# Gathered rows of a PEER layer taken in among its one-hot steps, on one Trainium2 core

## Chip, core and metric

One core of one Trainium2 chip runs the whole program. The metric is device microseconds, the median of several executions; a difference below about 0.2% can't be told from none. Engines are TensorE (PE in the profile), VectorE (DVE), ScalarE (ACT), GpSimd (POOL) and SyncE (SP), which issues most DMAs.

## What is computed

Two transformer blocks over 512 tokens of width 1024, ending in a feed-forward layer with 16384 experts. Only this layer (`peer_block`) is touched:

```python
q = (xb @ w_q).reshape(T, 8, 2, 128)
s = einsum('thpd,hpkd->thpk', q, sub_keys)        # 128 keys per half
sv, si = top_k(s, 16)
cand, cidx = sums and index pairs of the 16 x 16 candidates
top_s, pos = top_k(cand, 16)                      # 8 heads x 16 experts per token
gate = softmax(top_s)
u = take(expert_u, eidx); act = gelu(einsum('thkd,td->thk', u, xb))
v = take(expert_v, eidx); out = einsum('thk,thkd->td', gate * act, v)
```

Here T is the tokens, h the heads, k the 16 chosen experts.

## The kernel before

The layer is done in two ways. For the first 128 tokens (`GT`) the 128 chosen rows of `expert_u` and then the 128 of `expert_v` are gathered by indirect DMAs, one row per token and DMA (128 x 1024 floats, 0.5 MB): GpSimd issues them (`row_load`, L2847), VectorE reduces each (`gd`, L2598: a multiply with a sum for `expert_u`, a multiply-add for `expert_v`). That makes 256 rows, in four buffers `grow`, loaded three ahead.

For the other 384 tokens (`SD`) all experts are computed: 128 blocks of `expert_u` (128 experts each) are multiplied with the tokens, passed through Gelu, multiplied by a gate matrix that is zero except for the chosen experts, and multiplied with `expert_v`. Weights are loaded by SP into three ring buffers (`load_to`). Every fp32 weight block is split into a high and a low part: ScalarE copies it as the high part (`hi`, L1302 to L1306), the low part is the difference, made by GpSimd (`lo_to`, L2691 to L2697) or VectorE (`lo`, L1803 to L1806) as `by_pool` says. TensorE does three matmuls per product (`mm3`, L804 to L806). Up to the block `FIRST` there are three slots (`SLOTS`) for split blocks: `hi(n)` waits until TensorE has used block n - 3 (`slot_before`); after it there are eight.

The order of the work is one list, `ORDER`, written by `schedule`; each engine walks it and does its own part of every piece, in that order. `walk` also calls, after every piece in `one_unit` ("pre" is one), the engine's split function for two blocks ahead:

```python
for name, *args in ORDER:
    if name in pieces:
        pieces[name](*args)
    if name in one_unit:
        split_to(args[-1] + 2)
```

The stages, in order:
- Routing (`cand`, `best`, `gates`, `decode`, `look`, `sums`, `soft`, four blocks of 128 tokens): VectorE finds the chosen experts. `soft(0)` gives `eidx`, the indices of the gathered rows. Among this TensorE does `pre` pieces: `pre(j)` is block j of `expert_u` (24 matmuls of 384 columns), whose Gelu ScalarE writes to a tile that SP stores to DRAM (`zd`). There are 80 `pre` in all; 20 (`SOFT`) are done before `oh_begin`.
- One-hot (`hot(tb)`, 24 steps of 16 tokens): VectorE makes five bf16 products of 128 x 2048 (L2571, L2573, three times L2576), TensorE 48 matmuls (L1212) that turn them into gate rows, ScalarE moves those to a staging tile (L1707, four times a step), SP stores a piece of `TG` = 64 tokens every fourth step (`gd`, six pieces of 4 MB). Two `pre` stand before each `hot`; 52 `pre` (`HOT`) are in this stage, four of them before the first `hot`.
- Passage: after `ex_begin` (all engines wait for all) eight `pre`, the first gate loads (`gload`), `xtok` (the first 128 tokens turned to rows, `gx`, on TensorE and ScalarE), `gfirst` (the first three row loads), and `z(0)`.
- Expert loop, c = 0 to 31 with four blocks each: `z(c, j)` multiplies the stored (c < 20) or just computed (c >= 20) Gelu by the gates on VectorE (L2589), ScalarE and GpSimd split the result (L1728, L2843), `v(c, j)` multiplies it with a block of `expert_v` (18 matmuls of 512 columns). `feed(share)` puts `gd` pieces in between: 1.2 per `v` up to c = 18, then 1.8 per `z` and 1.8 per `v`.

Of the kernel before, what the change touches and what calls it, by code (L numbers as in the profile page):

```python
# [23 lines left out]
TG = 64  # L24
# [12 lines left out]
SOFT = 4 + 4 * 4  # L37
HOT = 4 + 48
# [109 lines left out]
def placed(items, kind):  # L148
    assert len(items) == len(PLACES[kind])
    return list(zip(PLACES[kind], items))  # L150


def schedule():
# [300 lines left out]
def build(nc, t):  # L454
    ORDER, UNITS, FIRST, OF = schedule()
    NU = len(UNITS)
    with ExitStack() as ctx:
# [168 lines left out]
        a = Stage("oh")  # L626
        iom = a(128 * QT, BF16)
# [7 lines left out]
        a = Stage("ex")  # L635
        exw = a(2048)
# [3 lines left out]
        gall = a(2 * JC * SD)  # L640
# [4 lines left out]
        grows = a(GR * 1024)  # L645
        gx = a(1024)
# [26 lines left out]
        whole = {n for n, (name, _) in enumerate(UNITS) if name == "ada"}  # L673
        halved = [n for n in range(FIRST) if n not in whole]
# [623 lines left out]
        def scalar_program(act):  # L1298
# [479 lines left out]
            def xg(k):  # L1778
# [14 lines left out]
                  **{f"{s}_begin": lambda s=s: fence(w, A, s) for s in ("rw", "eo", "at", "ao", "mx", "pk", "oh", "ex")}}, hi_to)  # L1793

        def vector_program(dve):
# [867 lines left out]
            def last():  # L2663
                w.wait_ge(tensor_done, T("bc", "ng"))
                for k in range(KT):
# [13 lines left out]
                  "yms": yms, "wo": wo, "wq": ahead_of, "keys": keys, "pre": lambda j, n: lo_to(n + 1), "cand": cand_,  # L2679
# [4 lines left out]
        def pool_program(pool):  # L2684
            w = Once(pool)
            at = {"lo": 0}
# [159 lines left out]

            def row_load(e):  # L2847
                if e >= NG:
                    return
# [5 lines left out]
                pool.indirect_dma_start(grow[e % GR], None, rows, bass.IndirectOffsetOnAxis(ap=at_, axis=0)).then_inc(  # L2855
                    grow_in[e % GR], 16)

            def gfirst():
                for s in st_out:
                    w.wait_ge(s, 16 * (SD // TG // 2))  # L2860
                for e in range(GR - 1):
                    row_load(e)
# [4 lines left out]
                  "pre": ahead_of, "z": z, "v": v, "gfirst": gfirst, "gd": lambda e: row_load(e + GR - 1),  # L2867
# [302 lines left out]
```

## Time and profile before

| | us |
|---|---|
| median of 3 runs | 2854.35 (2854.25 to 2856.07) |
| the profiled execution, its own time | 2859.36 |
| its span | 2857.5 |
| TensorE busy | 2697.9 (94%) |
| VectorE busy | 2213.6 (77%) |
| GpSimd busy | 1298.4 (45%) |
| ScalarE busy | 1212.2 (42%) |
| mean granted TensorE clock | 0.981 |

The sums cover stages with different limits, so each stage is to be read alone. The page also gives the busy share over 40 slices of 71 us; the routing stage, the one-hot stage and the passage are slices 22 to 28, the expert loop is 28 to 38:

```
PE   8889999999999999999999799999999999998987
DVE  3688888876878977657569998883777788888975
DMA  7321111134422221023233346677999999899961
```

### The profile page before, as it was taken

What the parts mean: (1) busy time and instruction counts of PE and PEld (TensorE: products, weight loads), DVE (VectorE), ACT (ScalarE), POOL (GpSimd) and SP (SyncE); (2) the same over time, 40 slices, a digit from 0 to 9 for tenths busy, and PEclk for the clock granted to TensorE, in tenths of its full rate; (3) what the DMA queues carried; (4) which work ended last, traced back from release to release, by engine and by line L of the source; (5) the groups of instructions that cost most, each with busy time, mean ns of one, the idle gap of its engine ahead of it and who ended that gap; (6) DMA issues with size and microseconds to landing.
All of it is one profiled execution on the core that took longest, in us unless ns stands there. A gap on an engine that the chain in (4) does not pass through costs nothing.

```text
span 2857.5 us, 36824 instructions
## 1 busy us (share of the span) xinstructions
PE 2697.9 (94%) x14355; PEld 2240.7 (78%) x14355; DVE 2213.6 (77%) x3528; ACT 1212.2 (42%) x1802; POOL 1298.4 (45%) x827
## 2 busy tenths in 40 slices
PE   8889999999999999999999799999999999998987
PEld 4567777767767788787788799999888898777765
DVE  3688888876878977657569998883777788888975
ACT  4234444443533466733334446564333333233333
POOL 2233333332224544204444455555676766667730
PEclk9999999999999999999999899999999999999998
DMA  7321111134422221023233346677999999899961
GB/s 280 103 70 53 52 52 52 52 125 151 144 67 74 82 67 45 30 83 117 82 103 103 119 133 225 209 249 278 360 377 361 376 341 340 321 337 322 325 246 37
DMA packets 163165, 496.12 MB, mean 174 GB/s; under 512 B 15152, under 2 KB 50992, under 8 KB 162864
## 3 DMA queue, kind: packets, MB, share of 16 engines
q1 hardware_dynamic: 126128, 359.53, 37.2%
q0 software_dynamic: 36864, 134.23, 12.7%
q8 instruction: 114, 1.87, 0.3%
q14 instruction: 59, 0.48, 0.0%
HBM read 443.90 MB, written 49.81 MB: 173 GB/s over the span
## 4 chain that ended last, share of the span: by engine, by line
PE 50%; DVE 24%; DMA 12%; ACT 7%; issue 4%; POOL 3%; SPq 1%; DVEq 0%; ACTq 0%; POOLq 0%
PE ps L804 12%; PE ps L806 12%; PE ps L805 12%; DMA ex<-in_ev,small 4%; DMA ex<-in_urow,small 4%; DVE ex L1806 3%; PE ps L1212 2%; DVE ex L2589 2%; DVE ex L2603 2%; DVE ex L2610 2%; DVE wsp L1806 2%; PE ps L977 2%; POOL ex L2843 1%; PE ps L997 1%; DMA ring<-in_ev 1%
## 5 line engine op out<-in xcount | busy, mean ns | idle before, releaser
L2697 POOL TENSOR_TENSOR wsp<-ring,wsp 128x1024 fp32r<-128x1024 f32 x219 | 568.2, 2600 | 867.5 <-ACT wsp L1306 839.7
L804 PE MATMUL ps<-hT,wsp 128*128 128x512 f32 (+1 forms) x2040 | 780.7, 383 | 38.0 <-POOL wsp L2697 20.0
L806 PE MATMUL ps<-hT,wsp 128*128 128x512 f32 (+1 forms) x2040 | 752.4, 369 | 0.0
L805 PE MATMUL ps<-hT,wsp 128*128 128x512 f32 (+1 forms) x2040 | 752.0, 369 | 0.0
L804 PEld LDWEIGHTS ps<-hT,wsp 128*128 128x128 f32 x2040 | 388.4, 190 | 109.1 <-issue 32.1
L806 PEld LDWEIGHTS ps<-hT,wsp 128*128 128x128 f32 x2040 | 387.8, 190 | 46.7
L805 PEld LDWEIGHTS ps<-hT,wsp 128*128 128x128 f32 x2040 | 388.9, 191 | 44.0 <-issue 5.0
L1306 ACT ACTIVATE wsp<-ring 128x1024 fp32r<-128x1024 f32 x317 | 331.9, 1055 | 158.0 <-PE ps L806 80.0
L804 PE MATMUL ps<-ex 128*128 128x512 f32 x588 | 233.7, 397 | 30.4 <-DVE ex L1806 26.9
L2855 POOL DMA_INDIRECT ex<-in_ev,small x128 | 190.5, 1488 | 110.1 <-DVE ex L2610 93.1
L2855 POOL DMA_INDIRECT ex<-in_urow,small x128 | 197.1, 1540 | 88.6 <-DVE small L2603 77.3
L805 PE MATMUL ps<-ex 128*128 128x512 f32 x588 | 230.5, 392 | 0.0
L806 PE MATMUL ps<-ex 128*128 128x512 f32 x588 | 229.9, 391 | 0.0
L1306 ACT ACTIVATE ex<-ring 128x1024 fp32r<-128x1024 f32 x115 | 120.3, 1060 | 252.9 <-DMA ring<-in_ev 188.5
L2610 DVE SCALAR_TENSOR_TENSOR ex<-ex,small 128x1024 f32<-128x1024 f32 x127 | 171.5, 1351 | 40.7 <-DMA ex<-in_ev,small 31.0
L1806 DVE TENSOR_TENSOR ex<-ring,ex 128x1024 fp32r<-128x1024 f32 x115 | 175.3, 1526 | 34.8 <-ACT ex L1306 34.8
L1982 DVE SCALAR_TENSOR_TENSOR ps<-rw,vec,ps 128x512 f32<-128x512 f32 x232 | 173.4, 747 | 5.3
L2603 DVE CUSTOM_DVE_ANT_0 ex<-ex 128x1024 f32<-128x1024 f32 x128 | 159.0, 1253 | 23.4 <-DMA ex<-in_urow,small 23.0
L2576 DVE TENSOR_TENSOR oh<-oh,px 128x2048 bf16<-128x2048 bf16 x72 | 176.2, 2500 | 0.8
L804 PEld LDWEIGHTS ps<-ex 128*128 128x128 f32 x588 | 111.1, 189 | 63.9 <-DVE ex L1806 41.6
L2843 POOL TENSOR_TENSOR ex<-ex 128x384 fp32r<-128x384 f32 x128 | 143.0, 1136 | 37.4 <-ACT ex L1728 36.5
L1728 ACT ACTIVATE ex<-ex 128x384 fp32r<-128x384 f32 x128 | 64.8, 525 | 199.4 <-DVE ex L2589 199.4
(431 smaller groups left out, 4909.3 us busy)
## 6 DMA issues: line engine op xcount, KB each, us to landing
ring<-in_eu SPq DMA_DIRECT2D x128, 512.0 KB
ring<-in_ev SPq DMA_DIRECT2D x128, 512.0 KB
ring<-in_ein SPq DMA_DIRECT2D x57, 512.0 KB
gd<-oh SPq DMA_DIRECT2D x6, 4096.0 KB, 14.0
ex<-gd SPq DMA_DIRECT2D x32, 768.0 KB
ring<-in_oin SPq DMA_DIRECT2D x39, 512.0 KB
ring<-in_ada SPq DMA_DIRECT2D x30, 512.0 KB
ex<-zd SPq DMA_DIRECT2D x20, 768.0 KB, 9.9
```

The lines of the kernel that those rows point to most:

```text
L804: pe.matmul(out, W[0], R[0], start=first, stop=False)
L805: pe.matmul(out, W[0], R[1], start=False, stop=False)
L806: return pe.matmul(out, W[1], R[0], start=False, stop=last)
L1306: act.activation(split_of(n)[:, 0, :], raw_of(n), ACT.Copy).then_inc(scalar_done, A.step("hi", n))
L1806: dve.tensor_tensor(s[:, 1, :], raw_of(n), s[:, 0, :].bitcast(F32), ALU.subtract).then_inc(vector_done, V.step("lo", n))
L1982: dve.scalar_tensor_tensor(out=y, in0=u[:, k:k + S], scalar=col("conv_w", m * TAPS + k), in1=taps, op0=ALU.mult, op1=ALU.add).then_inc(vec ...
L2576: dve.tensor_tensor(by_two(g), by_two(oj), spread_(i, t0), ALU.mult).then_inc(vector_done, V.step("hot", tb))
L2603: dve.tensor_tensor_reduce(out=row, in0=row, in1=gx, scale=1.0, scalar=0.0, op0=ALU.mult, op1=ALU.add, accum_out=of).then_inc(vector_done, ...
L2610: dve.scalar_tensor_tensor(out=gx, in0=row, scalar=of, in1=gx, op0=ALU.mult, op1=ALU.add).then_inc(vector_done, V.step("g", e))
L2697: pool.tensor_tensor(s[:, 1, :], raw_of(i), s[:, 0, :].bitcast(F32), ALU.subtract).then_inc(pool_done, G.step("lo", i))
L2843: pool.tensor_tensor(agb[c % 2][:, 1, j, :], exg[2 + (c * JC + j) % 3], agb[c % 2][:, 0, j, :].bitcast(F32), ALU.subtract).then_inc(pool_d ...
L2855: pool.indirect_dma_start(grow[e % GR], None, rows, bass.IndirectOffsetOnAxis(ap=at_, axis=0)).then_inc(grow_in[e % GR], 16)
```

## The change

Seven things:
- 40 of the 256 rows (`EARLY`) are taken earlier: one `gd` after every `hot`, four after the last, twelve in the passage. Until then they use three buffers, two ahead (`AHEAD`); `row_slots` gives buffer, count and predecessor of each row. Fewer are left for the loop: `feed` shares of 0.95 and 1.58.
- `xtok` moves to the start of the routing stage, `gfirst` (two rows) behind its first block.
- `TG` is 48: eight stored pieces of 3 MB, one every third step.
- 28 `pre` in the routing stage rather than 20, 44 in the one-hot stage rather than 52 (five before the first `hot`, then one or two per `hot`).
- `by_pool` gives the low parts of blocks 33 to 71 to VectorE; its `pre` handler asks for block n rather than n + 1 there.
- The tiles are placed anew, so that `gx` and three row buffers are free from the routing stage on.
- ScalarE waits for the stores of the first staging tile at `ex_begin`, no longer in `xtok`; `gload` waits for the `zd` stores.

```diff
-TG = 64
+TG = 48
-SOFT = 4 + 4 * 4
-HOT = 4 + 48
+EARLY = 40
+AHEAD = 2
+SOFT = 6 + 5 + 5 + 6 + 6
+HOT = 5 + 24 + 15
+def row_slots():
+    late = [3, *((EARLY + i) % 3 for i in range(3))]
+    slot = [e % 3 if e < EARLY else late[(e - EARLY) % GR] for e in range(NG)]
+    nth = [slot[:e].count(slot[e]) for e in range(NG)]
+    before = [max((k for k in range(e) if slot[k] == slot[e]), default=-1) for e in range(NG)]
+    return slot, nth, before
...
     for _ in range(4):
         pre()
+    order.append(("xtok",))
+    for _ in range(2):
+        pre()
     for blk in range(4):
         order.append(("cand", blk))
         pre()
         for part in range(4):
             order.append(("best", blk, part))
-            if part in (1, 3):
+            if part:
                 pre()
...
         pre()
+        if blk > 1:
+            pre()
         order.append(("sums", blk))
         order.append(("soft", blk))
+        if blk == 0:
+            order.append(("gfirst",))
...
     order.append(("oh_begin",))
-    for _ in range(4):
+    for _ in range(5):
         pre()
     for tb in range(SD // TB):
         pre()
-        pre()
+        if tb % 8 in (1, 3, 5, 6, 7):
+            pre()
         order.append(("hot", tb))
+        early(1)
+    early(4)
...
     order.append(("ex_begin",))
     pre()
+    early(2)
     pre()
+    early(1)
     order.append(("gload", 0))
     pre()
+    early(2)
     order.append(("gload", 1))
     for _ in range(3):
         pre()
-    order += [("xtok",), ("gfirst",)]
+        early(2)
     order.extend(zs(0))
     pre()
+    early(1)
     pre()
...
-        share = 1.2 if c < NPRE - 1 else 1.8
+        share = 0.95 if c < NPRE - 1 else 1.58
...
-                    or name == "eu" and u < NPRE * JC)
+                    or name == "eu" and u < NPRE * JC and not SOFT + 5 <= u < SOFT + HOT)
...
+            def ex_begin():
+                fence(w, A, "ex")
+                w.wait_ge(st_out[0], 16 * (SD // TG // 2))
...
-                  "pre": lambda j, n: lo_to(n + 1), "cand": cand_,
+                  "pre": lambda j, n: lo_to(n if SOFT + 5 <= j < SOFT + HOT else n + 1), "cand": cand_,
...
-                if e >= GR:
-                    w.wait_ge(vector_done, V("g", e - GR))
+                if row_before[e] >= 0:
+                    w.wait_ge(vector_done, V("g", row_before[e]))
...
             def gfirst():
-                for s in st_out:
-                    w.wait_ge(s, 16 * (SD // TG // 2))
-                for e in range(GR - 1):
-                    row_load(e)
+                rows_to(AHEAD - 1)
...
-                  "gd": lambda e: row_load(e + GR - 1),
+                  "gd": lambda e: rows_to(e + (AHEAD if e < EARLY - 1 else GR - 1)),
...
             def gload(c):
+                for s in z_out:
+                    w.wait_ge(s, 16 * ((SOFT + HOT) // 2))
```

## Rows read from the trace of the kernel before

**Rows 1.** The page of before: its first line and section 1.

```profile
span 2857.5 us, 36824 instructions
...
PE 2697.9 (94%) x14355; PEld 2240.7 (78%) x14355; DVE 2213.6 (77%) x3528; ACT 1212.2 (42%) x1802; POOL 1298.4 (45%) x827
```

**Rows 2.** Windows cut at the stages (columns in the first line).

```profile
core 0: us, PE busy (x) PEld busy (x) DVE busy (x) ACT busy (x) POOL busy (x), PEclk, DMA share, GB/s
1549.00:1666.20 117.20, 91.19 (x496) 90.32 (x495) 111.95 (x419) 47.93 (x70) 50.77 (x20) 0.89 0.39 124
1691.00:1950.40 259.40, 259.40 (x2259) 255.78 (x2257) 220.16 (x113) 155.87 (x188) 142.12 (x46) 1.00 0.65 211
1950.40:1992.00 41.60, 37.08 (x224) 36.47 (x223) 6.51 (x7) 17.03 (x25) 21.28 (x13) 1.00 0.92 333
1992.00:2304.00 312.00, 311.92 (x1354) 255.43 (x1355) 245.03 (x324) 112.62 (x152) 221.29 (x163) 0.99 0.98 367
2304.00:2744.00 440.00, 404.88 (x2002) 357.63 (x2001) 387.26 (x352) 139.39 (x189) 300.11 (x214) 1.00 0.92 330
```

**Rows 3.** Timeline of VectorE, 1985 to 1995 (start us, us, engine, line).

```profile
1989.32 2.36 DVE L1806 TENSOR_TENSOR ex<-ring,ex 128x1024 fp32r<-128x1024 f32 x2 [1.54 <-ACT ex L1306]
```

**Rows 4.** The chain that ended last (start us, us, what).

```profile
1936.40 2.77 PE ps L1212 x48
...
1947.55 2.77 PE ps L1212 x48
...
2019.34 7.83 DMA ex<-in_urow,small
```

**Rows 5.** Timeline of ScalarE, and of GpSimd for 1953.43.

```profile
1623.61 0.49 ACT L1673 ACTIVATE pk<-ps 128x384 f32<-128x384 f32 x1 [2.72 <-PE ps L806]
...
1627.77 0.49 ACT L1673 ACTIVATE pk<-ps 128x384 f32<-128x384 f32 x1 [2.72 <-PE ps L806]
...
1948.30 3.82 ACT L1707 ACTIVATE oh<-ps 128x512 f32<-128x512 f32 x4 [0.21 <-PE ps L1212]
1952.20 1.06 ACT L1306 ACTIVATE wsp<-ring 128x1024 fp32r<-128x1024 f32 x1
...
1953.43 2.39 POOL L2697 TENSOR_TENSOR wsp<-ring,wsp 128x1024 fp32r<-128x1024 f32 x1 [6.10 <-ACT wsp L1306]
```

**Rows 6.** The line of the one-hot products on VectorE.

```profile
L2576 DVE TENSOR_TENSOR oh<-oh,px x72: 1209/3408/3429, 1676.4 to 1934.9; 128x2048 bf16<-128x2048 bf16 x72
```

**Rows 7.** Windows of 5 us, 1985 to 2000.

```profile
1985.00:1990.00 5.00, 3.80 (x22) 3.48 (x21) 3.01 (x2) 2.19 (x3) 3.36 (x4) 1.00 0.87 351
1990.00:1995.00 5.00, 2.92 (x7) 2.38 (x8) 4.10 (x6) 3.39 (x7) 2.21 (x3) 0.71 0.64 207
1995.00:2000.00 5.00, 5.00 (x22) 4.08 (x22) 5.00 (x4) 2.54 (x3) 4.85 (x3) 0.95 1.02 405
```

**Rows 8.** Timeline of TensorE: `xtok`.

```profile
1976.74 3.73 PE L1224 MATMUL ps<-ident,hT 128*128 128x128 f32 x32
```

**Rows 9.** Timeline of VectorE, routing stage: where blocks 2 and 3 begin.

```profile
1612.99 0.98 DVE L2466 TENSOR_TENSOR pk<-pk 128x128 f32<-128x128 f32 x5
...
1637.92 0.98 DVE L2466 TENSOR_TENSOR pk<-pk 128x128 f32<-128x128 f32 x5
```

**Rows 10.** Windows of routing blocks 1 and 2.

```profile
1591.80:1613.00 21.20, 7.08 (x41) 6.76 (x40) 20.50 (x89) 3.86 (x6) 4.86 (x2) 0.76 0.33 104
1613.00:1637.90 24.90, 18.79 (x99) 18.50 (x99) 24.17 (x88) 10.60 (x16) 9.92 (x4) 0.91 0.37 116
```

**Rows 11.** Groups by form, VectorE, 2305 to 2745.

```profile
L2610 DVE SCALAR_TENSOR_TENSOR ex<-ex,small 128x1024 f32<-128x1024 f32 x124 | 167.1, 1348 | 40.4 <-DMA ex<-in_ev,small 31.0 <-DVE wsp L1806 0.3
...
L2603 DVE CUSTOM_DVE_ANT_0 ex<-ex 128x1024 f32<-128x1024 f32 x41 | 54.0, 1329 | 12.2 <-DMA ex<-in_urow,small 12.1
```

**Rows 12.** Timeline, 2545 to 2550: GpSimd's issue, and VectorE beside it.

```profile
2547.29 1.93 POOL L2855 DMA_INDIRECT ex<-in_ev,small  x1 [1.96 <-DVE ex L2610]
...
2545.73 2.68 DVE L2610 SCALAR_TENSOR_TENSOR ex<-ex,small 128x1024 f32<-128x1024 f32 x2
```

More of the change, by code:

```diff
@@ L380, in schedule, with early @@
         pre()
+        if blk > 1:
+            pre()
         order.append(("sums", blk))
         order.append(("soft", blk))
+        if blk == 0:
+            order.append(("gfirst",))
+    row = [0, 0.0]
+    def early(n):
+        for _ in range(n):
+            order.append(("gd", row[0]))
+            row[0] += 1
     assert z[0] == SOFT
     order.append(("oh_begin",))
-    for _ in range(4):
+    for _ in range(5):
         pre()
@@ L403, in schedule @@
         pre()
-    order += [("xtok",), ("gfirst",)]
+        early(2)
     order.extend(zs(0))
     pre()
+    early(1)
     pre()
+    assert row[0] == EARLY
     assert z[0] == NPRE * JC
     first = len(units)
-    row = [0, 0.0]
     def feed(share):
@@ L626, in build @@
         a = Stage("oh")
+        a(4 * 1024)
         iom = a(128 * QT, BF16)
@@ L635, in build @@
         a = Stage("ex")
+        gall = a(2 * JC * SD)
+        gr = a((GR + 1) * 1024)
         exw = a(2048)
@@ L673, in build @@
         whole = {n for n, (name, _) in enumerate(UNITS) if name == "ada"}
+        row_slot, row_nth, row_before = row_slots()
         halved = [n for n in range(FIRST) if n not in whole]
@@ L1792, in scalar_program @@
                   "v": v, "xtok": xtok, "gact": gact, "vl": vl, "vev": vev, "vtr": vtr, "pp": lambda m: pp(m) if m < 2 else None, "ple": lambda m, n: hi_to(n + 2), "ple_ev": ple_ev, "ple_end": ple_end, "xg": xg,
-                  **{f"{s}_begin": lambda s=s: fence(w, A, s) for s in ("rw", "eo", "at", "ao", "mx", "pk", "oh", "ex")}}, hi_to)
+                  **{f"{s}_begin": lambda s=s: fence(w, A, s) for s in ("rw", "eo", "at", "ao", "mx", "pk", "oh")}, "ex_begin": ex_begin}, hi_to)
         def vector_program(dve):
@@ L2598, in gd @@
             def gd(e):
-                row, of = grow[e % GR], gact_[:, e % 128:e % 128 + 1]
-                w.wait_ge(grow_in[e % GR], 16 * (e // GR + 1))
+                row, of = grow[row_slot[e]], gact_[:, e % 128:e % 128 + 1]
+                w.wait_ge(grow_in[row_slot[e]], 16 * (row_nth[e] + 1))
                 if e < NG // 2:
@@ L2678, in vector_program @@
                   "pool_in": ahead_of, "mx_begin": mx_begin, "pool_ev": pool_ev, "bc": bc, "res": res, "vc": vc,
-                  "yms": yms, "wo": wo, "wq": ahead_of, "keys": keys, "pre": lambda j, n: lo_to(n + 1), "cand": cand_,
+                  "yms": yms, "wo": wo, "wq": ahead_of, "keys": keys, "pre": lambda j, n: lo_to(n if SOFT + 5 <= j < SOFT + HOT else n + 1), "cand": cand_,
                   "best": best, "gates": gates, "decode": decode, "look": look, "soft": soft, "hot": hot, "z": z, "v": v, "gd": gd, "gact": gact, "vl": vl, "vtr": vtr,
@@ L2685, in pool_program @@
             w = Once(pool)
-            at = {"lo": 0}
+            at = {"lo": 0, "row": 0}
             def own():
@@ L2845, in gated, with rows_to @@
                     pool_done, G.step("ag", c, j))
+            def rows_to(n):
+                while at["row"] <= min(n, NG - 1):
+                    row_load(at["row"])
+                    at["row"] += 1
             def row_load(e):
-                if e >= NG:
-                    return
                 w.wait_ge(vector_done, V("eidx"))
-                if e >= GR:
-                    w.wait_ge(vector_done, V("g", e - GR))
+                if row_before[e] >= 0:
+                    w.wait_ge(vector_done, V("g", row_before[e]))
                 rows = t["urow"][:, :] if e < NG // 2 else t["ev"].rearrange("i j d -> (i j) d")
                 at_ = eidx[:, e % 128:e % 128 + 1].bitcast(U32)
-                pool.indirect_dma_start(grow[e % GR], None, rows, bass.IndirectOffsetOnAxis(ap=at_, axis=0)).then_inc(
-                    grow_in[e % GR], 16)
+                pool.indirect_dma_start(grow[row_slot[e]], None, rows, bass.IndirectOffsetOnAxis(ap=at_, axis=0)).then_inc(
+                    grow_in[row_slot[e]], 16)
             def gfirst():
-                for s in st_out:
-                    w.wait_ge(s, 16 * (SD // TG // 2))
-                for e in range(GR - 1):
-                    row_load(e)
+                rows_to(AHEAD - 1)
             walk({"ada": ahead_of, "dense": dense_part, "norm_nf": norm_nf, "mix": mix,
@@ L2866, in pool_program @@
                   "qi": qi_, "key": key, "keyhi": keyhi, "value": ahead_of, "q": ahead_of, "turnq": turnq, "qhi": qhi, "gate": ahead_of, "quiet": quiet, "ogs": ogs,
-                  "pre": ahead_of, "z": z, "v": v, "gfirst": gfirst, "gd": lambda e: row_load(e + GR - 1),
+                  "pre": ahead_of, "z": z, "v": v, "gfirst": gfirst, "gd": lambda e: rows_to(e + (AHEAD if e < EARLY - 1 else GR - 1)),
                   **{f"{s}_begin": lambda s=s: fence(w, G, s) for s in ("rw", "eo", "at", "ao", "mx", "pk", "oh", "ex")}}, lo_to)
```

4 lines of the change are left out of this document (1 added, 3 removed).

## The prediction, made before the changed kernel ran

> **What bounds the kernel now.** I read the page's first section, then the windows cut at the stages, then in each stage the view that names its limit. [Rows 1]: the profiled span is 2857.5 us and TensorE is busy 94% of it, so time can only come from the places where it waits. [Rows 2] show these. In the routing stage (1549 to 1666) TensorE is busy 91.2 of 117.2 us at a granted clock of 0.89, and VectorE 112: the top-k blocks hold it. In the one-hot stage (1691 to 1950) TensorE is busy throughout and sets the pace; VectorE has 39 us of slack. The passage to the expert loop (1950 to 1992) is 41.6 us with the DMA share at 0.92. The first part of the expert loop (to 2304) is TensorE's again: 312 us for 76 `v` pieces, 4.1 us each. In the last part (to 2744) TensorE is idle 35 us, and DMA (0.92) and VectorE (88%) are both near full.
>
> **Two facts of the code that decide.** First, `walk` calls the split function with n + 2 after every `pre`, since "pre" is in `one_unit`; the handler's own n or n + 1 is overtaken by that. The trace shows it on VectorE: between the products of `z(0)` and of `z(1)` stand two low parts together [rows 3], where the handler's n + 1 alone would give one. So the edit of VectorE's `pre` handler does nothing, and at `pre(j)` VectorE makes the low part of block j + 2. Second, there are three split slots, so the high part of j + 2 waits until TensorE has used j - 1, and the low part waits for the high part.
>
> **Before**, these low parts are on GpSimd, beside everything. **After**, blocks 33 to 71 have theirs on VectorE, in program order: at step tb VectorE first makes the low part of jl + 2 (jl is the last block ahead of `hot(tb)`), and only then the five one-hot products of `hot(tb)`, for which TensorE waits. Those products can no longer run ahead. That is the wait that the change adds; behind it on VectorE are the products and the row's reduction, and TensorE waits for the products.
>
> **One-hot steps, term by term.** Now a step is two blocks and one `hot`: 11.15 us from one `hot` to the next, of which `hot` is 2.8 [rows 4]. A block is 4.16 us (from one Gelu to the next, [rows 5]).
> A product costs VectorE 1209 ns with GpSimd silent, and up to 3429 beside a GpSimd subtraction [rows 6]; GpSimd will have no subtraction here, so five cost 6.05. A low part costs 1.2 (two in 2.36, [rows 3]).
> A step with one block ahead of its `hot` (steps 2, 4, 8, 10, 12, 16, 18 and 20): ScalarE must first move out the last `hot`, which ends 4.57 us after that `hot` began (1952.12 against 1947.55), then makes the high part; a low part can begin at 1953.43, 5.88 us after [rows 4, 5]. Then 1.2 + 6.05 + 0.2 of signals: 13.3 us from `hot` to `hot`.
> A step with two blocks (15 of them): 2.8 + 4.16 to the use of block jl - 1, 0.2, then Gelu 0.49 and high part 1.06 (some 0.1 of them overlapped, [rows 5]), 0.2, low part 1.2, products 6.05, 0.16: 16.2 us.
> Sum of the 23 steps: 8 x 13.3 + 15 x 16.2 = 349 us, against 23 x 11.15 = 256: **+93**. Ends: +85 if signals and evictions overlap better, +100 if they don't. For the first `hot` TensorE has used five blocks at 20.8 us; high part, low part and products follow until 29.3, where TensorE would be ready at 25.0: **+4**.
> The 24 row reductions in these steps (1.3 us each) fall where VectorE waits for ScalarE, 5.9 us per step: 0. If that cover were gone, 31 us. Their loads are two steps ahead, some 28 us, against a landing of about 8 [rows 4]: 0. The stores in eight pieces rather than six are 768 bytes a packet and the same sum of bytes, at a lower demand per us than the DMA share of 0.65 of now [rows 2]: they hide, 0.
>
> **The clock.** Each step now leaves TensorE idle 5 to 6 us. After an idle time of 1.2 + 2.1 us around 1990 the granted clock reads 0.71 and then 0.95 in two slices of 5 us [rows 7]: at 1.2 GHz for a part, 5 x 0.29 + 5 x 0.05 = 1.7 us lost. The work that follows a gap is `hot`, which stands on the chain. 24 x 1.7 = **+41**; ends 0 (the clock stays at 2.4 GHz) and +65 (2.7 each).
>
> **Routing stage.** Eight more blocks here (28 for 20), and `xtok`, 3.7 us [rows 8]. TensorE's room is 26 us idle and some 5 of low clock, against 8 x 4.16 + 3.7 = 37: at least +6. But VectorE holds the stage. Its blocks begin at 1591.8, 1613.0 and 1637.9 [rows 9]: 21.2 us beside two low parts of GpSimd, 24.9 beside four [rows 10], so 1.85 per low part. Blocks 1, 2 and 3 go from two, four, four to about six each: 7.4 + 3.7 + 3.7 = **+15** (6 to 20). The two row loads after block 0 hold GpSimd's queue until `eidx` (1591.8) and 3 us more; it has then split up to block 11, which TensorE ends at 1549 + 12 x 4.16 + 3.7 = 1602.6, so nothing waits.
>
> **Passage to the expert loop.** `xtok` leaves (-3.7), the last store is a quarter smaller. But rows 26 to 39 stand here, in three slots, two ahead: three rows per landing (8 us), GpSimd's issue and low part between (4) and reduction (1.3), some 4 us a row. The fence of all engines now takes in row 27. GpSimd's low parts 74 to 79 stand behind row issues that wait for VectorE, and `z(0)` stands behind row 38. Stepped through, `v(0)` starts 57 us after the last `hot`, where it is 41.6 now [rows 2]: **+16** (0 to +25).
>
> **Expert loop.** First part: TensorE sets it, fewer rows change nothing: 0. Last part: 440 us, where 48 pairs of a block and a `v` piece need 48 x 8.26 = 396. Rows here go from 165 to 144. On VectorE 21 rows take 21 x 1.35 = 28 with them, and their share of the 43 us that it waits for row transfers, 5 [rows 11]: -33. By bytes, 21 x 0.524 MB of 145 MB at 330 GB/s is 33 us too. **-32**; ends -15 (the low parts' own waits on transfers stay) and -44 (the floor).
>
> **Sum**: 93 + 4 + 41 + 15 + 16 - 32 = +137. The profiled execution took 2859.4 us, 5.0 over the median of 2854.35; the difference is set on the median: 2991.
>
> **A rule weighed.** A row issue of GpSimd reads its indices in SBUF. [Rows 12]: an issue of 1.93 us stands beside two VectorE operations with two SBUF inputs that last 2.68 together, 1.34 each, as everywhere (mean 1348 ns in [rows 11]); so issues hold nothing up. The Trainium skill (SBUF — State Buffer, "Who interferes with whom") says that a VectorE instruction with two SBUF inputs contends with a GpSimd instruction that reads SBUF, and that the one that starts first keeps the port pair for its whole length. By that rule the issues too could block products; for the subtractions the trace agrees, for the issues it doesn't.
>
> **Rivals.**
> A. The low parts don't hold the products back, because high parts come earlier than I read. Then TensorE sets the steps: 8 x 7.0 + 15 x 11.15 = 223, -33; no clock loss; -33 + 15 + 16 - 32 = -34: 2820, **faster**. For it: the counts of blocks per step fit VectorE's work (6.05 + 1.63 x 1.2 + 1.3 = 9.3 us) to TensorE's 9.6. Against it: the slots, and [rows 3]. It decides where the gap at each `hot` is under 1.4 us.
> B. The clock stays at 2.4 GHz through the gaps, as it does in the last part, at 1.00 with 35 us idle in all [rows 2]: 2950.
> C. Row issues block the products after all, 24 x 1.4 us (0.94 to 1.93): +34, 3025. Against: [rows 12], and that an issue follows a reduction, when VectorE is idle.
> D. A, but with the passage at +25 and the last part giving nothing back: 15 - 33 + 25 = +7, about the same as before.
>
> **Chances.** Forecast 0.65, B 0.16, C 0.06, A 0.11, D 0.02. A measurement tells 0.2% (6 us) from no change; faster 0.11, same 0.02, slower 0.87. The range takes the low ends, 85 + 4 + 0 + 6 + 0 - 44 = +51, and the high ends, 100 + 4 + 65 + 20 + 25 - 15 = +199: 2905 to 3050. That holds B and C and leaves out A and D.
>
> **What would show it.** Right: in the changed profile `hot` to `hot` is 13 and 16 us by turns, TensorE waits some 5 us before L1212 on VectorE's products, a product falls to 1.2 us, the clock line dips in the one-hot slices, and the last part takes about 408 us. Wrong: `hot` to `hot` of 7 and 11 us with no idle time ahead of it (A), a clock of 1.00 there (B), or products well over 1.21 us (C). A last part of 440 us would say that rows did not matter there.

## The result and the profile after

The changed kernel takes 2963.96 us (2962.85 to 2965.5, four runs); the kernel before, on the same chip, 2855.21 (2854.25 to 2861.45, four runs). The ratio is 1.0375, 95% interval 1.0357 to 1.0393: slower by 3.75%, +108.75 us. Forecast were +137 and 2991, range 2905 to 3050.

The page of the changed kernel: span, section 1, four lines of section 2, two groups of section 5, one line of section 6. L1245 is the one-hot matmul, L1841 VectorE's low part, L1339 ScalarE's high part, L2606, L2608 and L2611 the one-hot products, L2638 the row reduction, L2893 the row issue, L837 to L839 `mm3`, L1740 ScalarE's move of the gate rows.

```profile
span 2962.2 us, 36778 instructions
...
PE 2723.1 (92%) x14355; PEld 2273.0 (77%) x14355; DVE 2176.5 (73%) x3567; ACT 1213.3 (41%) x1802; POOL 1163.2 (39%) x788
...
PE   8889999999999999999999967667799999999987
...
DVE  3688888877869977567598755556677777889875
...
PEclk9999999999999999999999998898899999999998
DMA  7221111134422211132325454555999988999971
...
L1841 DVE TENSOR_TENSOR wsp<-ring,wsp 128x1024 fp32r<-128x1024 f32 x137 | 172.1, 1257 | 201.3 <-ACT wsp L1339 201.2
...
L1245 PE MATMUL ps<-oh 128*128 128x128 bf16 x1152 | 100.9, 267 | 108.1 <-DVE oh L2611 108.1
...
gd<-oh SPq DMA_DIRECT2D x8, 3072.0 KB, 11.4
```

Against [rows 1]: five slices of the one-hot stage, at 9 before, read 6 and 7 for TensorE, and VectorE has fallen there as well (5 and 6). When both engines are idler than before, neither is the bound: each waits for the other in turn. L1841 names the first wait (201 us on ScalarE's high part, 151.8 of them in the one-hot stage, 36 times), L1245 the second (108 us on the last product).

Windows of the changed kernel at its stages: two routing blocks, one-hot stage, passage, and the two parts of the expert loop (columns as in [rows 2]).

```profile
1557.50:1600.00 42.50, 42.50 (x259) 42.50 (x258) 31.14 (x91) 17.38 (x26) 22.20 (x9) 1.00 0.52 164
1600.00:1624.50 24.50, 17.40 (x99) 16.79 (x97) 23.82 (x88) 9.89 (x13) 15.63 (x7) 0.93 0.61 193
...
1717.00:2077.00 360.00, 256.37 (x2011) 249.40 (x2010) 207.45 (x200) 144.30 (x167) 24.75 (x24) 0.89 0.53 168
2078.00:2137.00 59.00, 42.10 (x241) 40.55 (x239) 33.76 (x38) 18.72 (x26) 40.59 (x28) 0.88 0.92 340
2137.00:2456.00 319.00, 319.00 (x1393) 261.87 (x1392) 230.68 (x299) 112.08 (x153) 205.12 (x150) 1.00 0.92 347
2456.00:2844.00 388.00, 380.89 (x1933) 345.48 (x1932) 343.33 (x293) 135.89 (x186) 259.10 (x184) 1.00 0.91 329
```

In the one-hot stage TensorE is idle 104 of 360 us, where it was idle 0 of 259 [rows 2]; the granted clock falls from 1.00 to 0.89. The last part now has TensorE idle 7 us, where it was 35.

The same stages by their boundaries, in us, for the profiled execution of each kernel ("loop, last" is from the first to the last Gelu of the expert loop, "loop, first" the stretch from `v(0,0)` to the first of these). The experiments are told below.

| | first `hot` at | 23 steps | last `hot` to `v(0,0)` | loop, first | loop, last | last Gelu to first `vev` | median of runs |
|---|---|---|---|---|---|---|---|
| before | 1690.9 | 256.5 | 44.7 | 319.6 | 423.2 | 34.9 | 2855.2 |
| after | 1716.7 | 361.1 | 58.6 | 319.7 | 387.5 | 33.6 | 2964.0 |
| e1_lows_gpsimd | 1712.8 | 240.3 | 58.3 | 319.4 | 383.8 | 32.7 | 2842.7 |
| e2_lows_in_time | 1719.1 | 223.3 | 60.6 | 320.2 | 383.8 | 33.0 | 2827.0 |
| e3_only_lows | 1697.5 | 388.0 | 43.9 | 319.7 | 427.8 | 36.3 | 2998.2 |
| e4_no_rows_in_passage | 1712.9 | 223.3 | 46.7 | 318.0 | 388.9 | 50.2 | 2830.6 |
| e5_shares | 1714.7 | 223.2 | 46.7 | 318.0 | 392.1 | 31.3 | 2810.6 |
| e6_routing_order | 1710.2 | 223.3 | 47.7 | 318.0 | 384.9 | 33.9 | 2805.8 |
| e7_twenty_in_routing | 1688.9 | 256.5 | 60.1 | 320.0 | 386.7 | 33.3 | 2833.1 |
| e8_only_pieces | 1688.3 | 256.5 | 42.3 | 318.0 | 424.8 | 33.3 | 2854.6 |
| e9b_short_reductions | 1691.4 | 256.5 | 44.8 | 319.7 | 383.2 | 30.1 | 2816.6 |
| e10b_short_rows | 1687.8 | 256.5 | 44.8 | 319.6 | 394.6 | 35.9 | 2830.1 |

From before to after: +25.8, +104.6, +13.9, +0.1, -35.7, -1.3, together +107.4, and -2.7 behind the first `vev`: the spans differ by 104.7. (Routing takes 27.7 us longer, and its stage begins 1.9 us earlier, at 1557.5 for 1559.4. This start lies between 1556.2 and 1563.8 over the twelve profiles, ahead of the pieces that were moved, so the first column holds some us of chance.) The medians differ by 4 us more, as the profiled execution of before was above its median.

**One step, read closely.** The chain that ended last, in the changed kernel, over a step with one block (from 1733.97) and one with two (from 1747.65).

```profile
1733.97 2.75 PE ps L1245 x24
1736.74 1.63 ACT oh L1740 x2
1738.53 1.16 ACT oh L1740
1739.69 0.86 ACT wsp L1339
1740.58 1.23 DVE wsp L1841
1741.80 1.13 DVE oh L2606
1742.93 1.15 DVE oh L2608
1744.10 3.50 DVE oh L2611 x3
1747.65 4.33 PE ps L1245 x48
...
1756.63 1.06 ACT wsp L1339
1757.72 1.23 DVE wsp L1841
1758.94 1.14 DVE oh L2606
1760.08 1.15 DVE oh L2608
1761.25 3.50 DVE oh L2611 x3
1764.80 2.75 PE ps L1245 x24
```

Every step goes round one loop: TensorE, ScalarE's high part, VectorE's low part, five products, TensorE. With one block it takes 13.7 us, with two 17.1, and each engine in it waits for the one before. In the one-block step the way from TensorE to the high part leads through the evictions of `hot`; in the other through the first of the two blocks, whose use until 1756.2 frees the slot that the high part of 1756.63 goes to; the second block runs beside the rest. VectorE's own timeline has the wait.

```profile
1740.58 1.23 DVE L1841 TENSOR_TENSOR wsp<-ring,wsp 128x1024 fp32r<-128x1024 f32 x1 [5.52 <-ACT wsp L1339]
...
1747.52 1.22 DVE L2638 CUSTOM_DVE_ANT_0 ex<-ex 128x1024 f32<-128x1024 f32 x1
```

The 5.52 us of idle time before the low part is where VectorE made its products ahead in the kernel before. The row reduction (1747.52) fits beside `hot` and costs the chain nothing.

### The profile page after: what moved, and what is told of

It reads as the page before. It is cut to its first block, busy times and chain, and to the rows that moved or that the text cites. A ratio compares the mean times of both kernels' runs of the same rounds, so it can differ in the third digit from the quotient of the medians.

```text
span 2962.2 us, 36778 instructions
## 1 busy us (share of the span) xinstructions
PE 2723.1 (92%) x14355; PEld 2273.0 (77%) x14355; DVE 2176.5 (73%) x3567; ACT 1213.3 (41%) x1802; POOL 1163.2 (39%) x788
## 4 chain that ended last, share of the span: by engine, by line
PE 59%; DVE 21%; DMA 7%; ACT 7%; issue 3%; POOL 2%; SPq 1%; DVEq 0%; ACTq 0%; POOLq 0%
PE ps L837 15%; PE ps L839 15%; PE ps L838 15%; DMA ex<-in_ev,small 4%; PE ps L1245 3%; DVE oh L2611 3%; DVE ex L1841 2%; DVE ex L2645 2%; DVE wsp L1841 2%; DMA ex<-in_urow,small 2%; PE ps L1010 1%; ACT wsp L1339 1%; PE ps L1030 1%; DVE ex L2624 1%; PE ps L984 1%
## 5 line engine op out<-in xcount | busy, mean ns | idle before, releaser
L837 PE MATMUL ps<-hT,wsp 128*128 128x512 f32 (+1 forms) x2040 | 782.2, 383 | 41.2 <-POOL wsp L2732 23.7
L839 PE MATMUL ps<-hT,wsp 128*128 128x512 f32 (+1 forms) x2040 | 754.2, 370 | 0.0
L2732 POOL TENSOR_TENSOR wsp<-ring,wsp 128x1024 fp32r<-128x1024 f32 x180 | 443.4, 2467 | 749.5 <-ACT wsp L1339 723.9
L837 PEld LDWEIGHTS ps<-hT,wsp 128*128 128x128 f32 x2040 | 389.6, 191 | 111.3 <-issue 29.9
L839 PEld LDWEIGHTS ps<-hT,wsp 128*128 128x128 f32 x2040 | 388.8, 191 | 46.8
L838 PEld LDWEIGHTS ps<-hT,wsp 128*128 128x128 f32 x2040 | 390.2, 191 | 43.9 <-issue 5.0
L1339 ACT ACTIVATE wsp<-ring 128x1024 fp32r<-128x1024 f32 x317 | 332.3, 1056 | 161.4 <-PE ps L839 80.1
L2893 POOL DMA_INDIRECT ex<-in_urow,small x128 | 185.9, 1452 | 403.8 <-DVE small L2638 389.9
L1841 DVE TENSOR_TENSOR wsp<-ring,wsp 128x1024 fp32r<-128x1024 f32 x137 | 172.1, 1257 | 201.3 <-ACT wsp L1339 201.2
L837 PE MATMUL ps<-ex 128*128 128x512 f32 x588 | 230.8, 393 | 12.9 <-ACT ex L1706 6.8
L2893 POOL DMA_INDIRECT ex<-in_ev,small x128 | 188.8, 1475 | 109.3 <-DVE ex L2645 94.3
L839 PE MATMUL ps<-ex 128*128 128x512 f32 x588 | 229.4, 390 | 0.0
L1339 ACT ACTIVATE ex<-ring 128x1024 fp32r<-128x1024 f32 x115 | 120.0, 1060 | 208.8 <-DMA ring<-in_ev 143.6
L1245 PE MATMUL ps<-oh 128*128 128x128 bf16 x1152 | 100.9, 267 | 108.1 <-DVE oh L2611 108.1
L2645 DVE SCALAR_TENSOR_TENSOR ex<-ex,small 128x1024 f32<-128x1024 f32 x127 | 169.7, 1336 | 36.1 <-DMA ex<-in_ev,small 24.6
L2638 DVE CUSTOM_DVE_ANT_0 ex<-ex 128x1024 f32<-128x1024 f32 x128 | 173.5, 1359 | 28.6 <-DMA ex<-in_urow,small 28.6
L1841 DVE TENSOR_TENSOR ex<-ring,ex 128x1024 fp32r<-128x1024 f32 x115 | 166.5, 1449 | 31.9 <-ACT ex L1339 31.8
L1245 PEld LDWEIGHTS ps<-oh 128*128 128x128 bf16 x1152 | 96.7, 123 | 115.5 <-DVE oh L2611 115.3
```

The source lines that it names most:

```text
L837: pe.matmul(out, W[0], R[0], start=first, stop=False)
L838: pe.matmul(out, W[0], R[1], start=False, stop=False)
L839: return pe.matmul(out, W[1], R[0], start=False, stop=last)
L1245: r = pe.matmul(out[:, q * 128:(q + 1) * 128], pairs(o[0])[:, tk // QT, :, tk % QT], pairs(o[1 + m])[:, tk // QT, :, tk % QT], start=m == ...
L1339: act.activation(split_of(n)[:, 0, :], raw_of(n), ACT.Copy).then_inc(scalar_done, A.step("hi", n))
L1841: dve.tensor_tensor(s[:, 1, :], raw_of(n), s[:, 0, :].bitcast(F32), ALU.subtract).then_inc(vector_done, V.step("lo", n))
```

## Experiments

**Who holds the products: the low parts, or their place in the order?** Two edits of the changed kernel, and one of the kernel before. In the first, GpSimd makes the low parts again:

```diff
-                    or name == "eu" and u < NPRE * JC and not SOFT + 5 <= u < SOFT + HOT)
+                    or name == "eu" and u < NPRE * JC)
```

> The changed kernel with all low parts of the first 80 blocks back on GpSimd; everything else of the change stays. Theory (VectorE's low part of block jl + 2 holds the one-hot products back): the products run ahead again, no 5 us wait of TensorE before each one-hot step. But a GpSimd subtraction again stretches a product from 1.2 to up to 3.4 us, by 2.0 us per low part, so that VectorE needs 6.05 + 1.63 x 2.0 + 1.3 = 10.6 us per step against TensorE's 9.6: 23 steps in about 246 us instead of 361, the kernel at 2964 - 115 = 2849. Rival (the steps are long because of the row reductions and row issues among them, or the low clock): steps stay near 361 us and the kernel above 2940.

Measured: 2842.68 us (2836.7 to 2846.79), ratio to before 0.9955 (0.9941 to 0.9968). The steps fall from 361.1 to 240.3 us: 120.8 of the 127.3 us that lie between the two profiled spans (the medians are 121.3 apart). The first `hot`, with no low part ahead of its products, comes 3.9 us earlier, and the last part of the loop is 3.7 shorter. Without that one line the change is a small gain. It isn't free: steps vary from 6.99 to 13.86 us, 17 us more in all than in the next experiment. A product (L2611) beside a subtraction takes up to 3.44 us instead of 1.21, and TensorE waits four times for the last one, 10.5 us. Timelines of VectorE and of GpSimd in this kernel, a reduction and the subtraction beside it:

```profile
1821.70 3.42 DVE L2638 CUSTOM_DVE_ANT_0 ex<-ex 128x1024 f32<-128x1024 f32 x1
```

```profile
1821.18 2.86 POOL L2732 TENSOR_TENSOR wsp<-ring,wsp 128x1024 fp32r<-128x1024 f32 x1 [5.51 <-ACT wsp L1339]
```

In the second VectorE keeps the low parts, but `walk` no longer calls for them two blocks ahead; at `pre(j)` VectorE makes the low part of block j itself. `lo_after` takes the place of `lo_to` as the split function of VectorE's `walk`:

```diff
+            def lo_after(n):
+                name, u = UNITS[n - 2]
+                if name == "eu" and SOFT + 3 <= u < SOFT + HOT:
+                    lo_to(n - 2)
+                else:
+                    lo_to(n)
```

> The changed kernel, with VectorE making the low part of block j at pre(j) in the one-hot stage, not that of j + 2: the split function's call two blocks ahead is left out there. Same operations, same engines, one order changed. Theory: the high part of block jl is there long before, so the products follow at once; TensorE sets the steps again (7.0 and 11.15 us), 23 steps in 223 to 235 us, the clock stays at 1.00, the kernel at 2964 - 130 = 2834 (2824 to 2845). Rival (VectorE is simply too full: five products, 1.6 low parts, a row): steps of 15 us on average stay, 2964.

Measured: 2827.0 us (2825.78 to 2829.65), ratio 0.9901 (0.9884 to 0.9917), 137 us under the changed kernel. VectorE in this kernel, one step with two blocks (L2618 is the product that was L2611, L2645 the row reduction that was L2638):

```profile
1829.01 1.22 DVE L1841 TENSOR_TENSOR wsp<-ring,wsp 128x1024 fp32r<-128x1024 f32 x1
1830.88 1.23 DVE L1841 TENSOR_TENSOR wsp<-ring,wsp 128x1024 fp32r<-128x1024 f32 x1 [0.65 <-ACT wsp L1339]
...
1834.41 3.50 DVE L2618 TENSOR_TENSOR oh<-oh,px 128x2048 bf16<-128x2048 bf16 x3
1837.83 1.22 DVE L2645 CUSTOM_DVE_ANT_0 ex<-ex 128x1024 f32<-128x1024 f32 x1
```

The same instructions with the same durations stand there as in the changed kernel; the wait before a low part is 0.65 us where it was 5.5. Steps take 11.15 and 6.99 us, TensorE's own pace, at 219 ns a matmul. It isn't the engine of the low parts that costs the time, but that VectorE asks for them two blocks early, when their slot is not free, with the products queued behind.

In the third the low parts alone go to VectorE, in the kernel before:

```diff
-                    or name == "eu" and u < NPRE * JC)
+                    or name == "eu" and u < NPRE * JC and not SOFT + 4 <= u < SOFT + HOT)
```

> The kernel before with one edit: the low parts of blocks 24 to 71 on VectorE. No rows, no other piece size. Theory: every step has two blocks, so each takes the 17.1 us that such steps take in the changed kernel instead of 11.15: 23 x 5.9 = +137, the first step +5: 2855 + 142 = 2997. Rival (it is the rows that make the steps long): no more than 2870.

Measured: 2998.18 us (2992.64 to 3003.73, two runs), ratio 1.0498 (1.0468 to 1.0529). All steps have two blocks and take 17.06 to 17.10, the last 12.49: 388 for 256.5 us. So the part by itself is enough, without rows, pieces or moved blocks.

**The rows in the passage.** From the second experiment, with the last twelve early rows given back to the loop (`EARLY = 28`, no `early` behind `ex_begin`):

```diff
-EARLY = 40
+EARLY = 28
...
-    early(2)
...
-    early(1)
```

> e2 (low parts in time) with the twelve rows of the passage left to the expert loop (28 early rows, not 40). Theory (the passage is 56 us instead of 42 since the low parts 74 to 79 and z(0) stand behind row loads): the passage falls back to about 42 us, -13; twelve rows more in the last part of the loop cost 12 x 1.6 = +19 at most: e2's time within 6 us, with the passage shorter and the last part longer. Rival (the passage is long because the stores and gate loads saturate the DMA engines): passage stays at 52 to 56 us, and the kernel is 10 to 19 us slower than e2.

Measured: 2830.56 us (2830.27 to 2831.63), ratio 0.9912 (0.9896 to 0.9929): no gain over 2827.0. The passage did fall, from 60.6 to 46.7 us, which shows its price of 14 us. But at the same shares of `feed` those rows were left over at the end: 50.2 us instead of 33.0 from the last Gelu to the first `vev`, 5.1 more ahead of it and 3.8 behind it, 26 us together. Against them stand the 13.9 of the passage, 2.2 in the loop's first part, and 6.2 of an earlier first `hot`, of which 5.8 are an earlier start of the routing stage (1558.0 for 1563.8), where the two kernels are the same. The next run feeds those rows in the first part of the loop, where TensorE hides them:

```diff
-        share = 0.95 if c < NPRE - 1 else 1.58
+        share = 1.1 if c < NPRE - 1 else 1.58
```

> e4 with the share of rows in the first part of the expert loop at 1.1 instead of 0.95, so that the twelve rows not taken in the passage are done before the loop's end (28 + 76 x 1.1 + 96 x 1.58 is over 256; e4 came to 252 and had rows left over, 50 us from the last Gelu of the loop to the first eviction after it, where e2 has 33). Theory: TensorE sets the first part, so the added rows are free there: that stretch falls back to 33 us, -17: 2814, 12 us below e2. Rival (the last part pays for them): 2826.

Measured: 2810.59 us (2807.79 to 2813.2), ratio 0.9835 (0.9821 to 0.9848), 20 us under the run before it. (The two ran on different chips, and the kernel before was 3.8 us slower on this one; by the ratios the step is 22 us.) The tail is back at 31.3, and the first part of the loop, at 318.0, shows nothing of the 11 more rows in it.

**The routing stage.** On top of that, four `pre` stand before the first block, then 5, 6, 6 and 7 in the blocks, and `xtok` comes behind `cand(0)`:

```diff
-SOFT = 6 + 5 + 5 + 6 + 6
+SOFT = 4 + 5 + 6 + 6 + 7
...
-    order.append(("xtok",))
-    for _ in range(2):
-        pre()
     for blk in range(4):
         order.append(("cand", blk))
+        if blk == 0:
+            order.append(("xtok",))
         pre()
...
-        if blk > 1:
+        for _ in range((0, 1, 1, 2)[blk]):
             pre()
```

> e5 with the same 28 blocks in the routing stage set otherwise: 4 before it, then 5, 6, 6, 7 (instead of 6, then 5, 5, 6, 6), and xtok behind the first cand. Theory: in routing block 0 of the changed kernel VectorE waits 5.5 us for ScalarE's copies of the indices and 5.2 us for its exponential, both queued behind Gelus that wait for TensorE; with two blocks and xtok less ahead of them the first hot comes 5 to 10 us earlier, the kernel at 2804 to 2809. Rival (TensorE is full there, 28 blocks take their 117 us in any order): no gain, 2814.

Measured: 2805.82 us (2804.9 to 2813.41), ratio 0.9833 (0.982 to 0.9847), which the runs don't tell apart from the one before. In the profile block 0 falls from 42.5 to 34.2 us, as meant, but block 1 takes 26.5 for 24.6 us, and from the start of block 3 to the first `hot` it is 61.5 for 57.3. The first `hot` comes 4.5 us earlier, of which 2.1 are an earlier start of the stage: the new order gives 2.4, not the 5 to 10 that were expected. The last run on routing goes back to 20 and 52 blocks, on the second experiment, with the `pre` calls of `schedule` set as before the change:

```diff
-SOFT = 6 + 5 + 5 + 6 + 6
-HOT = 5 + 24 + 15
+SOFT = 4 + 4 * 4
+HOT = 4 + 48
...
```

> e2 (low parts in time, 40 early rows) with the counts of blocks of before: 20 in the routing stage, 52 in the one-hot stage, two to a step. Theory: the routing stage falls back by 22 to 26 us (first hot at about 1695), the steps are 11.15 us each, 256.5 for 23, +33 against e2: 2827 + 33 - 24 = 2836. If the eight blocks fitted into the routing stage's idle time without cost, it would be 2860; if they gained nothing there, 2827.

Measured: 2833.11 us (2830.1 to 2835.77), ratio 0.9918 (0.9903 to 0.9934). The steps take 33.3 us more. The first `hot` comes 30.2 us earlier, of which 4.9 are an earlier start of the stage; the routing itself is 25.3 shorter, with block 0 at 30.0 us for 42.5. So moving eight blocks (8 x 4.16 = 33) into the routing stage gives 33 us and costs 25 of them: VectorE holds that stage, but it has no 33 us of TensorE's idle time to give.

**The pieces of 48.** `TG = 48` alone, in the kernel before.

> The kernel before with one edit: gate rows stored in pieces of 48 tokens, eight of 3 MB. Theory: the stores lie beside a TensorE that is never idle in that stage; only the last store, a quarter smaller, stands ahead of the first gate load: 0 to -3 us, 2852 to 2855. Rival (smaller packets of 768 bytes hold up the weight loads): steps of more than 11.15 us behind a store, 2860 or more.

Measured: 2854.56 us (2847.45 to 2863.68, ten runs) against 2858.56 (2850.95 to 2867.64) for the kernel before on that chip; ratio 0.9991 (0.9974 to 1.0007): no difference.

**What bounds the last part of the loop.** Two edits of the kernel before, each for the 128 `expert_v` rows. In the first the multiply-add reads and writes 128 columns of 1024; in the second the transfer brings 128 columns.

```diff
-                    dve.scalar_tensor_tensor(out=gx, in0=row, scalar=of, in1=gx, op0=ALU.mult, op1=ALU.add).then_inc(
+                    dve.scalar_tensor_tensor(out=gx[:, 0:128], in0=row[:, 0:128], scalar=of, in1=gx[:, 0:128], op0=ALU.mult, op1=ALU.add).then_inc(
```

> The kernel before, with the multiply-add of the 128 second-product rows done on 128 of 1024 columns (7/8 of that sum is left out; all transfers stay). Theory, that the last part is set by VectorE's reductions: its work there falls by 124 x 1.2 us, the stretch from the first to the last Gelu of the loop falls from 423 us to TensorE's floor of about 388, total 2820. Rival, that the rows' transfers set it: the stretch stays at about 423, total 2855.

```diff
-                pool.indirect_dma_start(grow[e % GR], None, rows, ...
+                pool.indirect_dma_start(grow[e % GR] if e < NG // 2 else grow[e % GR][:, 0:128], None, rows, ...
```

> The kernel before, with the transfers of the 128 second-product rows cut to 128 of 1024 columns (64 KB for 512 KB each; what the reduction adds in the other columns is whatever lies there). Theory, that VectorE's reductions set the last part: the stretch from the first to the last Gelu of the loop stays within 5 us of 423, total 2850. Rival, that the rows' transfers set it: the stretch falls to about 388, total 2820. If both this run and the one with short reductions fall to 388, either of the two is enough to relieve VectorE, since its waits for rows and its work add up on one engine.

Measured: 2816.55 us (two runs), ratio 0.9854 (0.9805 to 0.9903), and 2830.09 (three runs), ratio 0.9905 (0.9881 to 0.9929). The stretch falls from 423.2 to 383.2 and to 394.6; the 388 that both expectations call TensorE's floor is thus not the floor. Groups by form of VectorE from 2305 to 2700: the first line is of the kernel with short reductions.

```profile
L2610 DVE SCALAR_TENSOR_TENSOR ex<-ex,small 128x128 f32<-128x128 f32 x123 | 62.1, 505 | 122.6 <-DMA ex<-in_ev,small 115.8 <-issue 1.5 <-DVE ex L1806 0.6
```

The second is of the kernel with short transfers.

```profile
L2610 DVE SCALAR_TENSOR_TENSOR ex<-ex,small 128x1024 f32<-128x1024 f32 x120 | 159.3, 1327 | 12.6 <-DMA ex<-in_ev,small 0.2
```

With short reductions all transfers are there, VectorE stands 115.8 us before rows that haven't landed, and still TensorE is not held. With full reductions and short transfers these waits fall to 0.2 us (27.4 before, over the same window), and 29 of the 40 us are gained; VectorE is still busy 366.5 of 396 us. So neither the reductions nor the transfers are the bound alone: on VectorE's queue the work and the waits for rows add up, and cutting either relieves it. Windows from 2304 to 2700, the kernel with short reductions:

```profile
2304.00:2700.00 396.00, 392.78 (x1996) 357.14 (x1995) 260.53 (x351) 140.79 (x191) 262.76 (x214) 1.00 0.97 366
```

The kernel with short transfers:

```profile
2304.00:2700.00 396.00, 383.23 (x1939) 345.88 (x1938) 366.54 (x334) 135.46 (x184) 295.19 (x204) 1.00 0.64 211
```

TensorE is busy 392.8 us in the first, at a DMA share of 0.97, and 383.2 in the second, at 0.64. The lower share is the slower of the two.

## Why the prediction was right, and where its sum was off

The total was forecast 28 us too high. By terms: the steps and the clock together -29.4 (104.6 for 134), the first `hot` +6.8, the passage -2.1, the loop -3.6; what lies behind the loop, -4.0, was not forecast, and the profile of before was 4 us above its median. So the mechanism was right and two terms were off in size, the clock above all; the first `hot`, which was forecast too early, took back a quarter of it. (The high ends of the range add to 3053, where 3050 stands; nothing hangs on it.)

- **The inert handler, and the low parts two blocks ahead of the products.** Right: the chain shows it, and e2, which changes only this, takes the gaps away. How many gaps there were is in the view of everything on L1245 in the changed kernel; the second fence is the same view of L2611:

```profile
L1245 PE MATMUL ps<-oh x1152: 217/308/312, 1716.7 to 2080.5; 128*128 128x128 bf16 x192
...
  DVE oh L2611: 223.4, 46
```

```profile
L2611 DVE TENSOR_TENSOR oh<-oh,px x72: 1215/1217/1226, 1713.1 to 2071.0; 128x2048 bf16<-128x2048 bf16 x72
```

  The 46 waits are counted for matmuls and weight loads alike, so each of the 23 gaps is there twice: 108.1 us of TensorE's, 4.4 to 5.2 each.
- **Steps, 349 us and +93.** The two kinds of step are right: forecast 13.3 and 16.2, before the clock. Of the chain, the stretch from the low part to `hot` is 7.07 us, where the forecast had 7.41 (products follow each other at 1.14 us, not 1.21): -7 over 22 steps. One of the 15 two-block steps was counted wrong: the last takes 12.47 us, since two blocks ahead of it are blocks 72 and 73, whose low parts are GpSimd's: -3.7.
- **The clock, +41.** Right in kind, too large in size, and the term that failed. The clock falls in every step; the window of TensorE from 1745 to 1750 in the changed kernel:

```profile
1745.00:1750.00 5.00, 2.35 (x23) 2.35 (x24) 3.74 (x5) 0.85 (x1) 0.94 (x1) 0.73 0.24 93
```

  After 5.12 us of idle time the first 28 of the 48 matmuls of `hot` run at the lower level (1.2 GHz), 308 ns each and one every 107 ns; the last 18 are at the higher one again (2.4 GHz), 218 ns and one every 57. All 48 take 4.3 us instead of 2.93: 1.4 us, which is 28 x 0.05. (Over the 23 gaps it is the first 26 to 31, hence the mean of 267 ns in section 5.) In a two-block step all but 0.1 of that lies on the chain: 10.07 us from `hot` to the low part, where 8.81 were forecast. In a one-block step ScalarE's four evictions run beside the matmuls, and only half of the loss passes through: 6.61 for 5.88. So 14 x 1.26 + 8 x 0.73 = 23 us, not 24 x 1.7 = 41. The last step has the loss too, 1.3 us inside its 12.47, so 25 us in all. Of the 16 us between, some 7 are the size (1.4 for the 1.7 taken from [rows 7]), 2 are one gap too many (23 for 24), and 7 are what overlaps the slower work, which the forecast put on the chain whole. Sum of the steps: 349 - 7 - 4 + 23 = 361, as measured.
- **First `hot`, +15 and +4.** 25.8 were measured, or 27.7 from the start of the stage. Blocks 1, 2 and 3 take 3.3, 5.3 and 4.9 us more, 13.5 against 14.8 forecast, and from the stage's end to the first `hot` 4.1 more against 4 (e1 and e2, where no late low part stands there, give 4 back). Block 0 was put at nothing and takes 42.5 for 32.4 us. Timelines of ScalarE and then of VectorE in the changed kernel:

```profile
1575.56 0.49 ACT L1706 ACTIVATE pk<-ps 128x384 f32<-128x384 f32 x1 [2.72 <-PE ps L839]
1575.95 1.14 ACT L1713 ACTIVATE pk<-pk 128x512 bf16<-128x512 uint32 x2
```

```profile
1577.22 4.57 DVE L2531 TENSOR_TENSOR pk<-pk 128x2048 bf16<-128x2048 bf16 x2 [5.48 <-ACT pk L1713]
...
1598.60 0.29 DVE L2560 TENSOR_REDUCE pk<-pk 128x8 f32<-128x128 f32 x1 [5.19 <-ACT pk L1720]
```

  ScalarE's copy of the indices (L1713) stands in the order behind the Gelus of two more `pre` and behind `xtok`, and TensorE, busy all 42.5 us, gets to them late; the exponential (L1720) likewise. The step that failed is "TensorE's room" taken as one sum over the stage: in block 0 there was none (TensorE was busy 32.40 of its 32.40 us already), and 10 us went there. e6 and e7 bear this out: with two blocks fewer ahead of it block 0 is 8 us shorter, with one fewer in it besides 12.5.
- **Passage, +16.** 13.9. e4 gives the rows' price alone, 13.9 too. The 3.7 us that the forecast took off for `xtok` are not seen: without the rows the passage is 46.7 us in e4, 44.7 before, though the smaller last store alone takes off 2.4 (e8). What took their place is open.
- **Loop, first part, 0.** +0.1.
- **Loop, last part, -32.** -35.7. TensorE is still idle 7 us in 388; the floor, 396 in the forecast, is nearer 383 (e1, e2, e9b). e5 and e6, with the same shares, are 7 us apart, so the 4 us between forecast and measurement say nothing. That both VectorE's work and its waits count, as the sum had it, is what e9b and e10b show.
- **Costed at nothing**: reductions beside `hot`, row issues and stores. In the one-hot stage the chain holds none of them, and e8 shows the pieces.
- **Rivals.** A asked for gaps under 1.4 us; they are 4.4 and more. Its own price was sound, though: where e1 and e2 free the products, the times are 2843 and 2827, and A said 2820. B asked for a clock of 1.00; it is 0.89. C asked for products well over 1.21 us; the longest of L2611 is 1.226.

The rule weighed: row issues follow the reductions, and no product is longer. [Rows 12], on which the forecast leaned, has VectorE starting first, so it couldn't show what an issue that starts first does. e2 has the closer row, GpSimd's issue during the low part of 1829.01:

```profile
1829.36 1.68 POOL L2900 DMA_INDIRECT ex<-in_urow,small  x1 [6.40 <-DVE small L2645]
```

The low part stays at 1.22 us; the issue is stretched from 0.94 to 1.68. So the price falls on GpSimd, which had time. The Trainium skill (SBUF — State Buffer, "Who interferes with whom") lets the instruction that starts first keep the port pair; this row fits that with VectorE first, and the reduction of 3.42 us in e1 fits it with the subtraction first.

The other order, the issue first, fits it less well. Timelines of GpSimd and then of VectorE in the changed kernel, two places in the passage and in the loop:

```profile
2121.63 0.94 POOL L2893 DMA_INDIRECT ex<-in_urow,small  x1 [0.31 <-issue]
2122.59 2.38 POOL L2732 TENSOR_TENSOR wsp<-ring,wsp 128x1024 fp32r<-128x1024 f32 x1
...
2202.53 0.94 POOL L2893 DMA_INDIRECT ex<-in_urow,small  x1 [0.59 <-DVE small L2638]
```

```profile
2122.19 3.87 DVE L2638 CUSTOM_DVE_ANT_0 ex<-ex 128x1024 f32<-128x1024 f32 x1 [1.69 <-DMA ex<-in_urow,small]
...
2202.63 1.23 DVE L1841 TENSOR_TENSOR ex<-ring,ex 128x1024 fp32r<-128x1024 f32 x1 [0.37 <-ACT ex L1339]
```

At 2202.63 the low part starts 0.10 us after the issue and neither is longer than alone (0.94 and 1.23), so the issue alone doesn't hold VectorE. Nor does it in e1, where twenty products begin under an issue and none takes more than 1.23 us. At 2122.19, with a subtraction directly behind the issue, the reduction starts 0.40 us before that subtraction and still lasts 3.87, until 1.09 after its end. Fifteen low parts in the expert loop stand so too, and last 2.55 to 2.58 us. Why VectorE gives way there although it began first is not shown.

## What to carry to other kernels

Work that is moved to another engine is queued there in program order: before it moves, list what stands behind it in that order, find out which call really asks for it (here a general look-ahead overrode the handler that was edited), and ask only when its inputs are due; block j at `pre(j)` instead of two ahead was worth 137 us with not one instruction more or less. A loss of speed on one engine is to be followed along the chain, since work that overlaps it takes a part of it back. And what is taken out of a full place goes to the stage with slack, with the tail checked: some twelve rows cost 14 us in the passage, some 20 at the end and nothing that shows in the first part of the loop, and with them there the kernel (e5_shares, e6_routing_order) takes 2806 to 2811 us, 1.7% under the kernel before.

## What was not expected of the hardware

After each idle stretch of 4.4 to 5.2 us TensorE runs the first 26 to 31 matmuls of the next `hot` at the lower level (308 ns each; all 48 take 4.2 to 4.5 us), and the rest of them and the blocks behind at the higher one again (24 matmuls in 4.16 us, as before). Fall and return both come in every step of 14 to 17 us, 23 times in the changed kernel and 23 in the one with the low parts alone; the one `hot` without a gap ahead of it (2077.75) takes 2.92 us. The forecast had expected a mean loss of 1.7 us spread over what follows, with part of the gaps perhaps at no loss. Shorter gaps stand in e1, four of them; TensorE's timeline there, the idle time in brackets:

```profile
1751.40 4.46 PE L1245 MATMUL ps<-oh 128*128 128x128 bf16 x48 [2.19 <-DVE oh L2611]
...
1814.89 4.20 PE L1245 MATMUL ps<-oh 128*128 128x128 bf16 x48 [3.17 <-DVE oh L2611]
...
1878.57 5.30 PE L1245 MATMUL ps<-oh 128*128 128x128 bf16 x48 [3.32 <-DVE oh L2611]
...
1930.72 2.93 PE L1245 MATMUL ps<-oh 128*128 128x128 bf16 x48 [1.84 <-DVE oh L2611]
```

After 1.84 us nothing falls. After 2.19 us the first 31 matmuls are at the lower level; after 3.17 us the first 22 are at the higher level and the fall comes behind them; after 3.32 us all 48 are at the lower one, and the `hot` takes 5.30 us. So a gap of 2 us can cost as much as one of 5, and its length alone doesn't give the loss; four gaps are too few to say more.

And the DMA share says nothing about the bound by itself: at 0.97 over 396 us TensorE was idle 3 us (short reductions), at 0.92 it was idle 29 in the same window of the kernel before.
